# Attention scores contracted over all 128 rows, with q and k placed by DMAs of two engines, and a new order of the first five stages

## What is computed

```python
h = rmsnorm(x, norm_g[i])
proj = h @ w_in[i]                 # columns: three mixers, their gates, merge gates
ya = forgetting_attention(qa, ka, va, log_sigmoid(fa + b_forget)) * silu(za)   # 8 heads x 64
yb = nsa_attention(...) * silu(zb)  # 8 heads x 64: compressed + selected + window
yc = differential_attention(...) * silu(zc)   # 4 heads, two 64-wide maps each
merged = g0 * (ya @ w_br_a) + g1 * (yb @ w_br_b) + g2 * (yc @ w_br_c)
x = x + merged @ w_out
x = x + sigmoid(x @ w_ple_gate) * (p[i] @ w_ple)
...
s = einsum('bqhd,bkhd->bhqk', q, k) * 64 ** -0.5   # the scores; A adds c_q - c_k
```

## Time and profile before

| | us |
|---|---|
| median of 3 runs (1538.67 to 1542.2) | 1541.11 |
| the profiled execution | 1538.75 |
| its span, first to last instruction | 1536.9 |
| PE busy (7957 matmuls) | 1496.8 |
| DVE busy | 941.2 |
| ACT busy | 636.7 |
| POOL busy | 75.4 |

### The profile page before, as it was taken

The page is one execution under the profiler, slowest core; times in us unless marked ns, Lnnn a source line. Parts: engine busy times, 40 slices in busy tenths (PEclk is TensorE's granted clock), DMA queues, the critical chain, the costliest instruction groups (busy, mean ns, idle before and its releaser), DMA issues.

```text
span 1536.9 us, 22588 instructions
## 1 busy us (share of the span) xinstructions
PE 1496.8 (97%) x7957; PEld 1205.0 (78%) x7957; DVE 941.2 (61%) x2197; ACT 636.7 (41%) x1499; POOL 75.4 (5%) x80
## 2 busy tenths in 40 slices
PE   8999999999999999999999999999999999999997
PEld 6777777887787777888787787787887777778885
DVE  6866765655657776554576667655556677854544
ACT  6533434433344444343444334334334444434343
POOL 1000000000000010000100000000000011000011
PEclk9999999999999999999999999999999999999998
DMA  7223332222223333332342324222222233233321
GB/s 197 84 83 90 97 76 62 56 70 62 69 63 96 90 83 83 98 108 72 106 108 69 103 76 115 64 52 66 63 62 76 70 96 89 70 101 99 89 86 72
DMA packets 250301, 129.50 MB, mean 84 GB/s; under 512 B 45690, under 2 KB 245972, under 8 KB 250196
## 3 DMA queue, kind: packets, MB, share of 16 engines
q1 hardware_dynamic: 250196, 128.13, 31.2%
HBM read 118.67 MB, written 2.10 MB: 79 GB/s over the span
## 4 chain that ended last, share of the span: by engine, by line
PE 87%; DVE 6%; ACT 3%; issue 2%; DMA 0%; POOL 0%; SPq 0%; ACTq 0%; POOLq 0%; DVEq 0%
PE D L732 24%; PE D L734 22%; PE D L733 22%; PE Ob L920 7%; PE S L879 5%; PE T L898 4%; DVE w_lo L1293 2%; ACT w_hi L1059 1%; PE Mb L936 1%; ACT probs L1173 1%; PE Mb L846 1%; PE Ob L924 1%; PE Mb L813 1%; DVE y_lo L1627 1%; DMA acc<-in_x_dram 0%
## 5 line engine op out<-in xcount | busy, mean ns | idle before, releaser
L732 PE MATMUL D<-h_hi,w_hi 128*128 128x512 f32 x1264 | 542.1, 429 | 9.9 <-DVE zs L1444 3.7
L734 PE MATMUL D<-h_lo,w_hi 128*128 128x512 f32 x1264 | 495.9, 392 | 0.0
L733 PE MATMUL D<-h_hi,w_lo 128*128 128x512 f32 x1264 | 494.3, 391 | 0.0
L1293 DVE TENSOR_TENSOR w_lo<-raw,w_hi 128x512 fp32r<-128x512 f32 (+2 forms) x504 | 295.0, 627 | 310.9 <-ACT w_hi L1059 310.7
L1059 ACT ACTIVATE w_hi<-raw 128x512 fp32r<-128x512 f32 (+2 forms) x504 | 264.6, 572 | 306.7 <-PE D L734 305.4
L732 PEld LDWEIGHTS D<-h_hi,w_hi 128*128 128x128 f32 x1264 | 238.5, 189 | 69.3 <-issue 18.4
L1173 ACT ACTIVATE probs<-probs,nmax 128x128 f32<-128x128 f32 (+3 forms) x256 | 141.9, 555 | 355.0 <-DVE nmax L1545 354.9
L734 PEld LDWEIGHTS D<-h_lo,w_hi 128*128 128x128 f32 x1264 | 237.4, 188 | 52.9
L733 PEld LDWEIGHTS D<-h_hi,w_lo 128*128 128x128 f32 x1264 | 239.4, 189 | 30.8 <-issue 0.5
L1545 DVE CUSTOM_DVE_ANT_0 probs<-S,maskb 128x128 f32<-128x128 f32 (+3 forms) x256 | 115.1, 487 | 48.4 <-PE S L879 29.8
L540 DVE COPY pT<-T 128x128 f32<-128x128 f32 (+3 forms) x160 | 77.4, 486 | 48.0 <-PE T L898 47.5
(11 more groups left out here) (243 smaller groups left out, 1498.9 us busy)
## 6 DMA issues: line engine op xcount, KB each, us to landing
raw<-in_w_in_dram SPq DMA_DIRECT2D x124, 512.0 KB, 3.9
raw<-in_w_in_dram SPq DMA_DIRECT2D x32, 256.0 KB, 3.7
raw<-in_w_out_dram SPq DMA_DIRECT2D x16, 512.0 KB, 4.1
raw<-in_w_ple_gate_dram SPq DMA_DIRECT2D x16, 512.0 KB, 4.2
rs<-rx SPq DMA_DIRECT2D x80, 64.0 KB, 2.0
raw<-in_cmp_w_k_dram SPq DMA_DIRECT2D x8, 512.0 KB, 3.8
raw<-in_cmp_w_v_dram SPq DMA_DIRECT2D x8, 512.0 KB, 3.8
raw<-in_w_br_a_dram SPq DMA_DIRECT2D x16, 256.0 KB, 2.9
```

The lines of the kernel that those rows point to most:

```text
L732: pe.matmul(o, w_hi[:, sl, cs], hi[:, k, :], start=(k == 0), stop=False)
L733: pe.matmul(o, w_lo[:, sl, cs], hi[:, k, :], start=False, stop=False)
L734: ins = pe.matmul(o, w_hi[:, sl, cs], lo[:, k, :], start=False, stop=last)
L1293: TT(w_lo[:, sl, half], raw[:, ring(L, t, RAW), half], f(w_hi[:, sl, half]), ALU.subtract).then_inc(M["dve_lo"], 1)
```

## The change

It does the following.

- **Scores.** A head's q is stacked, hi on 64 partitions and lo on the other 64, and its k is laid on both halves, `k_hi` in one part of the arena and `k_lo` in the next. A head's scores are then two matmuls over 128 rows (in A a third for the forget gates, whose 0/1 selection now reads one set of rows), one head after the other, and each head waits only for its own bank.
- **Placing.** ACT and DVE write hi and lo of a tile into one shared buffer `new`; a new item `put` has two DMAs issued by SP and two by ACT bring them to their places: 64x512 for q, 64x1024 for k. `put_s` counts them; scores wait for it, and so does ACT before it writes `new` for the next tile. `put` stands 1 step after the end of a `qa` or `ka` tile and 12 after a rotated one.
- **Order.** The tiles of stages -1 to 3 stand in another order, the weights of the steps are gone, the second layer of the value compression comes later (12 and 16 steps), and in the last unit the transposes come one tick earlier.
- **Loads.** RAW is 3, and the load of tile t + 5 is an item of its own, 1 step after the end of tile t.
- Besides: `rb` is gone (POOL multiplies in place), `vbd` is set to zero once at the start, the copy of `ck` to rows 64 to 103 is gone, and ACT's and DVE's loops over i are written out.

```diff
-RAW = 4
+RAW = 3
...
-    st = {-1: [("va", 0), ("va", 1), ("va", 2), ("va", 3), ("fg", 0), ("qa", 0), ("ka", 0), ("qa", 1)]}
-    st[0] = [("kcb", 0), ("ka", 1), ("za", 0), ("w1k", 0)]
-    st[1] = [("qa", 2), ("ka", 2), ("w1k", 1), ("ksb", 0), ("w1k", 2), ("za", 1)]
-    st[2] = [("qa", 3), ("w1k", 3), ("ka", 3), ("za", 2), ("vcb", 0)]
-    st[3] = [("qb", 0), ("w1v", 0), ("kwb", 0), ("w1v", 1), ("za", 3), ("w1v", 2), ("vsb", 0), ("w1v", 3), ("vwb", 0)]
+    st = {-1: [("va", 0), ("va", 1), ("va", 2), ("va", 3), ("fg", 0), ("ka", 0), ("qa", 0), ("kcb", 0)]}
+    st[0] = [("ka", 1), ("w1k", 0), ("qa", 1), ("w1k", 1), ("za", 0)]
+    st[1] = [("ka", 2), ("w1k", 2), ("qa", 2), ("w1k", 3), ("za", 1), ("vcb", 0)]
+    st[2] = [("ka", 3), ("qa", 3), ("w1v", 0), ("vsb", 0), ("w1v", 1), ("za", 2), ("qb", 0)]
+    st[3] = [("w1v", 2), ("ksb", 0), ("w1v", 3), ("kwb", 0), ("za", 3), ("vwb", 0)]
...
+            if kind in ("qa", "ka"):
+                follow.append([1, ("put", t)])
             if kind in ROTATED:
                 follow.append([8, ("swap", t)])
                 follow.append([11, ("rot", t)])
+                follow.append([12, ("put", t)])
+            follow.append([1, ("load", t + RAW + 2)])
...
-                limit = tick - (3 if u == UNITS - 1 else 2 if branch(u) == "C" else 1)
+                limit = tick - (2 if branch(u) == "C" else 1)
...
-            want = max(g for g in range(len(weight)) if weight[g] * N <= (j + 1) * weight[-1])
+            want = (j + 1) * len(groups) // N
...
+        q_st = [[part(6 * b + h) for h in range(2)] for b in range(2)]
+        k_at = [2, 8, 12]
+        KS, KW = 0, 2
+        new = sb("new", [P, 2 * S], F32R)
+        new_hi, new_lo = new[:, 0:S], new[:, S:2 * S]
...
+        def places(kind, n):
+
+            if kind[0] == "q":
+                q = q_st[n % 2]
+                return [(q[h][half((h + part_) % 2), :], new[half(h), part_ * S:(part_ + 1) * S])
+                        for h in range(2) for part_ in range(2)]
+            at = k_at[{"ka": n % 2, "ksb": KS, "kwb": KW, "kc": (n + 1) % 2}[kind]]
+            return [(part(at + 2 * h, 2)[half(g), :], new[half(h), :]) for h in range(2) for g in range(2)]
...
+                            for h in range(2):
+                                if r >= 2:
+                                    pe.wait_ge(M["dve_max"], r - 1 + h)
+                                qx = q_st[b][h][:, i * P:n]
+                                k_hi, k_lo = keys(m, u, h)
+                                pe.matmul(Sc[h][:, 0:n], qx, k_hi[:, 0:n], start=True, stop=False)
+                                ins = pe.matmul(Sc[h][:, 0:n], qx, k_lo[:, 0:n], start=False, stop=m != "a")
+                                if m == "a":
+                                    hh = 2 * u + h
+                                    ins = pe.matmul(Sc[h][:, 0:n], selr[:, hh:hh + 1].to_broadcast([P, P]), ck[:, 0:n],
+                                                    start=False, stop=True)
+                                ins.then_inc(M["pe_s"], 1)
...
+                                if placed.after(t) > 1:
+                                    act.wait_ge(M["put_s"], 64 * (placed.after(t) - 1))
+                                A(new_hi, D[:], ACT.Copy, scale=QSCALE if kind == "qa" else 1.0).then_inc(M["act_evac"], 1)
...
+                        elif what == "put":
+                            split_done(M, act, it[1])
+                            for dst, src in places(*tiles[it[1]][:2])[1::2]:
+                                act.dma_start(f(dst), f(src)).then_inc(M["put_s"], 16)
```

237 lines of the change are left out of this document (102 added, 135 removed).

## The result

| | before | after |
|---|---|---|
| median, us | 1540.58 | 1564.96 |
| lowest to highest, us | 1538.67 to 1542.20 | 1561.89 to 1565.98 |
| the profiled execution: span, us | 1536.9 | 1562.7 |
| its mean granted TensorE clock | 0.997 | 0.987 |

The ratio is 1.0158 (95% interval 1.0142 to 1.0173): 24.3 us slower, where 18.6 us faster was forecast. The range, 1509 to 1535, misses it as well, and so does the sign.

What follows compares the result with a forecast made beforehand. The prediction took TensorE, busy 97% of the span, as the bound. Its terms, -21.8 - 2.1 + 7.7 + 2 - 2.8 = -17.0 us, took the profiled 1538.75 us to 1522 us, range 1509 to 1535.

Steps and rivals of the forecast that it cites:

- The score form (-23.9): Score groups as 128-row matmuls without entry or exit gaps: 21.8 us off in units 4 to 11, 2.1 in 0 to 3.
- The placing at unit 0 (+7.7): First scores of each layer wait for ka's, then qa's placing DMAs: 4.2 us in layer 0, 3.5 in layer 1.
- ScalarE and VectorE around the placing (+2): ACT waits for DVE's split and issues DMAs before exponentials, for qa and ka: 2 us on, between 0 and 19.
- from qb on: Placing of later tiles stands four or more steps ahead of ACT's next work for PE: costs nothing.
- New order (0): Reordered tiles, compression spread wider: about 6 us of waits per layer before and after, so nothing, 5 us either way.
- Fewer buffers for weights (0): Weights loaded one tile less ahead (RAW 3): loads still land in time, so nothing.
- The last unit one tick earlier (-2.8): Last unit: two more dense steps ahead of the transpose of y that waited 1.88 us, 2.8 us off in both layers.
- Rival 3: Score-group gaps belong to any score group, not the 64-row form, so they stay: slower, 1567 us; chance 0.06.
- Rival 1: PE also waits for placing at later unit starts or behind ACT's DMA issues: about 1532 us; chance 0.21.
- growth of the waits for exponentials by more than 5 us in units 0 to 3: Sign named beforehand that the prediction is wrong: waits for exponentials in units 0 to 3 growing over 5 us.

Runs made afterwards that it cites:

- e2: The changed kernel with the old score form back (three 64-row products per head, forget term in 64 rows): 1580.13 us, 16.2 us more than the changed kernel.
- e6: The kernel before with only the new order of tiles, groups dealt without weights, value compression's second layer later: 1542.94 us, ratio 1.0013 to the kernel before.
- e9: The changed kernel with three repairs: sync engine issues all placing DMAs, last unit's three ticks restored, ka0 ahead of fg0: 1529.12 us, ratio 0.9935 to before.
- e4: The changed kernel with all four placing DMAs of a tile issued by the sync engine, none by ScalarE: 1545.81 us, 17.4 us less than the changed kernel.
- e1: The changed kernel with the last unit's transposes again three ticks after their scores instead of two: 1556.59 us, 6.5 us less than the changed kernel.
- e12: The kernel before with 14 waits put in by hand, TensorE waiting for GpSimd operations ahead of branch tiles: 1578.73 us, ratio 1.0243 to before.
- e11: e9 with the copies of qa and ka ahead of the weight half and layer 0's sines one tile later: 1526.22 us, ratio 0.9906 to the kernel before.
- e3: The changed kernel with fg0 moved between ka0 and qa0 ahead of unit 0: 1558.38 us, 6.6 us less than the changed kernel.

## Why the prediction was wrong, step by step

**The score form (-23.9): right in mechanism, oversized.** The groups between dense steps gained what was forecast, to 0.07 us. But with the form put back (e2) the kernel lost 16.2 us, not 24. The single units say where. Units 4 to 7 were charged 7.3 us a layer; their lengths differ by 5.9 and 5.8 us between e2 and the changed kernel, and by 6.4 and 6.1 between e6 and e9, which have the same order. Units 8 to 10 were charged 2.7. There e6 and e9, in which ScalarE issues nothing, differ by 2.6 and 2.4, but e2 and the changed kernel, in which PE waits in unit 8, by only 1.2 and 0.4 us (in layer 1 the changed kernel has one clock fall more). So in units 4 to 10 the form is worth some 80 to 95% of its term, and less in a kernel where PE waits anyway. The sum took the gain of a group between two dense steps for all groups; why units 4 to 7 gain less than that was not measured.

**The placing at unit 0 (+7.7): right place, too small.** 6.88 - 0.89 = 6.0 and 5.6 us, 11.6 in all, against 4.2 and 3.5 forecast. In layer 0 the chain that was written down (ka's DMAs, then qa's copy, then qa's DMAs) is the one in the rows, and its last link came as forecast: qa landed 4.2 us after its first issue, where 4.0 was reckoned. The link that was too short is ka's: from the first issue to the last landing it took 6.9 us in layer 0 (56.67 to 63.54) and 7.5 in layer 1, where 5.9 was reckoned. In layer 0 its second piece went out earlier than forecast, at 57.24 and not 58.6, and ka still landed at 63.54 and not 61.5.

**ScalarE and VectorE around the placing (+2): the step that failed.** e4 measures 17.4 us. The prediction had the upper end, 19 us for qa and ka alone, and chose 2 near the lower end, "since the dense steps between an exponential and its transpose (0.69 us each) mostly cover a stall of this size". And it put "from qb on" at nothing, where unit 8 alone lost 3.7 us a layer. An engine that is idle 59% of its time was taken for one with room. The time that counts is the room in front of the next operation that PE waits for, and on ScalarE in unit 8 there was none: three operations at once stand behind the issue.

**New order (0): right.** e6 gives +2.0, within the 5 either way, and the T waits behind w1k0 that the text named are there.

**Fewer buffers for weights (0): right as far as seen.** No wait for weights over 0.61 us in units 0 to 11 after.

**The last unit one tick earlier (-2.8): wrong in sign.** e1 measures 6.5 us the other way. The step looked at the one wait at the end of the chain (y_q, 1.88 us) and not at what a tick less leaves in front of the T of unit 11: exponentials, then four operations of VectorE, then the transpose. It waited 2.11 us there, and y_q 2.20 instead of less.

**The clock: not in the prediction at all.** Each of the new waits of about 1.5 us and more can take a fall of 1.6 us with it (e12 and the table behind it), the long ones at the first scores more. The changed trace shows falls at six of them; others, 1.86 us at 928.69, 2.33 at 967.50, 2.11 at 601.50 and 2.20 at 615.77, show none.

**The account.** From before to after: form -16.2 (e2), three mistakes together +34.4 (e9: issues on ScalarE, the order of ka0 and fg0, the tick), order +2.0 (e6), and what is left of the first scores' waits in e9, 5.6 - 0.9 = +4.7. Sum +24.9, measured +24.3. The clock falls are inside these numbers. Each of the measured parts is good to 2 to 4 us, so that the sum closes to 0.6 is partly luck.

**The rivals.** Rival 3 forecast 1567, and 1565 was measured, for a reason that is not so: its point of decision, a 512-column group over 1.11 us, was not reached (0.91), and e2 goes the wrong way for it. Rival 1, waits at ScalarE's issues, named the largest part of the truth, but was priced at half its upper bound and without the tick and the clock. Of what was named beforehand as a sign that the forecast is wrong, growth of the waits for exponentials by more than 5 us in units 0 to 3 came true, just: 0.64 + 1.39 us became 3.45 + 3.45 in unit 0 and 0.19 + 0.19 in unit 1.

## What to carry to other kernels

Before a DMA goes to a compute engine's queue, look at the room in front of the next thing on that queue that the bottleneck waits for, not at that engine's idle share: 88 issues, 58 us in all on an engine 59% idle, cost 14 to 17 us of span. A buffer shared by two tiles in a row turns their DMAs into a chain; something that another engine needs anyway goes between the two (6.6 us here), or a second buffer, which no run here tried. And where a change makes the bound engine wait, charge a wait of about 1.8 us or more at its length plus the clock it may cost, and test each part alone: this change held one gain of 16 us and three losses, and with those turned back (e9) and two more moves at the start (e11) it runs 0.94% under the kernel before.

## What the runs showed of the hardware

- The granted TensorE clock fell to 1.2 GHz behind waits as short as 1.50 us (ended at 439.46 in e3, granted 0.68 from 440 to 445). A fall costs about 1.6 us beyond the wait (e12); at the first scores of the changed kernel it lasts longer. It does not follow every time: 2.55 us in e12 had none, and the same wait in unit 2 had one in layer 0 and none in layer 1. The executions of one kernel differ by it too: of the kernel before, beside e1, the one of 1537.67 us has a mean granted clock of 0.997, the one of 1542.35 us 0.994.
- DMAs from SBUF to SBUF of 256 KB landed after 4.0 us when the sync engine issued them and 5.0 when ScalarE did, 128 KB after 2.6 and 3.1; each issue held ScalarE 0.58 us in the median (88 of them, 0.47 to 2.63, 58 us in all). Four from one issuer were in place no later than two and two: ka 6.7 and 6.8 us after the first issue in e4, 6.9 and 7.5 in the changed kernel, qa 4.15 against 4.2 and 4.1.
